# Fixed places for weight chunks, row counts in five steps, and a later fold in the last step of a mixture-of-experts block

## What is computed

```python
logits = h @ router_w + router_b                 # 512 tokens, 32 experts
top_vals, top_idx = lax.top_k(logits, 4)
gates = softmax(top_vals)
u = h[tokens of e] @ w_up[e] + b_up[e]           # 1024 -> 2048
a = min(u[::2], 7) * sigmoid(1.702 * min(u[::2], 7)) * (clip(u[1::2], -7, 7) + 1)
y = a @ w_down[e] + b_down[e]                    # 1024 -> 1024
x[tokens of e] += gate * y
out = rmsnorm(x) * final_norm_g
```

## Time and profile before

| | |
|---|---|
| runs | 1398.98, 1404.44, 1404.75 us; median 1404.44 |
| the profiled execution | 1400.33 us, its span 1398.5 us |
| TensorE busy | 94% of the span |
| VectorE busy | 85% |
| ScalarE busy | 75% |
| GpSimd busy | 20% |
| granted TensorE clock, mean | 0.979 |
| moved by DMA | 457.92 MB |

### The profile page before, as it was taken

The page is one execution under the profiler, slowest core; times in us unless marked ns, Lnnn a source line. Parts: engine busy times, 40 slices in busy tenths (PEclk is TensorE's granted clock), DMA queues, the critical chain, the costliest instruction groups (busy, mean ns, idle before and its releaser), DMA issues.

```text
span 1398.5 us, 18794 instructions
## 1 busy us (share of the span) xinstructions
PE 1311.2 (94%) x6287; PEld 1059.7 (76%) x6288; DVE 1185.3 (85%) x1064; ACT 1055.6 (75%) x900; POOL 281.0 (20%) x140
## 2 busy tenths in 40 slices
PE   6999989989998999999999999999999999999992
PEld 5888866678776878888788877778788878787771
DVE  5566645578998899999999999999999999999975
ACT  6454334336787898988889898989898888989873
POOL 0000001110165323322122121121122312212310
PEclk9999999989999999999999999999999999999996
DMA  8522153226999999999999999999999999999964
GB/s 243 143 61 76 46 199 163 94 103 252 406 337 408 371 411 412 409 414 397 420 400 416 405 420 403 398 402 414 416 405 408 407 413 406 421 404 408 399 248 140
DMA packets 71415, 457.92 MB, mean 327 GB/s; under 512 B 7371, under 2 KB 36203, under 8 KB 46737
## 3 DMA queue, kind: packets, MB, share of 16 engines
q1 hardware_dynamic: 64560, 438.13, 77.2%
q0 software_dynamic: 6816, 19.30, 5.8%
HBM read 443.35 MB, written 18.48 MB: 330 GB/s over the span
## 4 chain that ended last, share of the span: by engine, by line
PE 65%; DMA 16%; DVE 10%; issue 5%; ACT 3%; DVEq 0%; POOL 0%; SPq 0%; POOLq 0%; ACTq 0%
PE psum L1856 40%; DMA w_raw_pair<-w_up 11%; PE psum L1614 8%; DVE w_low L1258 5%; PE psum L1611 3%; DMA residual_rows<-y_rows,scatter_rows 3%; ACT w_high L777 2%; PE psum L1700 2%; PE psum L1748 2%; PE psum L1849 1%; PE psum L1839 1%; PE psum L1902 1%; DMA w_buf<-w_out 1%; PE psum L1724 1%; PE psum L1872 1%
## 5 line engine op out<-in xcount | busy, mean ns | idle before, releaser
L1258 DVE TENSOR_TENSOR w_low<-w_raw_pair,w_high 128x2048 fp32r<-128x2048 f32 x382 | 854.1, 2285 | 61.0 <-ACT w_high L777 60.1
L777 ACT ACTIVATE w_high<-w_raw_pair 128x2048 fp32r<-128x2048 f32 x384 | 717.8, 1911 | 117.2 <-DMA w_raw_pair<-w_up 45.6
L1856 PE MATMUL psum<-w_high,x_high 128*128 128x512 f32 x1040 | 286.3, 397 | 22.2 <-DVE x_high L1441 17.8
L1856 PE MATMUL psum<-w_low,x_high 128*128 128x512 f32 x1040 | 281.3, 392 | 0.0
L1856 PEld LDWEIGHTS psum<-w_high,x_high 128*128 128x128 f32 x1040 | 194.0, 190 | 71.1 <-DVE w_low L1258 27.4
L1856 PEld LDWEIGHTS psum<-w_low,x_high 128*128 128x128 f32 x1040 | 197.0, 189 | 42.2
L583 POOL DMA_INDIRECT residual_rows<-y_rows,scatter_rows x32 | 126.5, 3953 | 340.0 <-ACT y_rows L815 338.4
L1856 PE MATMUL psum<-w_high,a_high 128*128 128x512 f32 x496 | 156.2, 396 | 0.0
L1856 PE MATMUL psum<-w_low,a_high 128*128 128x512 f32 x496 | 154.2, 392 | 0.0
L1856 PE MATMUL psum<-w_high,x_low 128*128 128x512 f32 x512 | 141.1, 397 | 1.7 <-DVE w_low L1258 1.2
L1856 PEld LDWEIGHTS psum<-w_high,x_low 128*128 128x128 f32 x512 | 93.4, 188 | 26.8 <-issue 4.8
(11 more groups left out here) (306 smaller groups left out, 1451.4 us busy)
## 6 DMA issues: line engine op xcount, KB each, us to landing
w_raw_pair<-w_up SPq DMA_DIRECT2D x128, 2048.0 KB, 16.0
w_raw_pair<-w_down SPq DMA_DIRECT2D x64, 2048.0 KB, 14.9
w_in_raw<-w_in SPq DMA_DIRECT2D x28, 512.0 KB, 3.8
w_buf<-w_out SPq DMA_DIRECT2D x2, 2048.0 KB, 11.1
x_rows<-x SPq DMA_DIRECT2D x4, 512.0 KB, 5.4
x_rows<-x SPq DMA_DIRECT2D x1, 2048.0 KB, 18.8
residual_rows<-x_rows SPq DMA_DIRECT2D x4, 512.0 KB, 2.6
normed_rows<-h_rows SPq DMA_DIRECT2D x4, 512.0 KB, 2.6
```

Of the source, the lines that this page charges most:

```text
L777: act.activation(wh[:, q.slot(m, SPL), :], raw[q.slot(m, RAW)][:, :], ACT.Copy).then_inc(wh_ready, 1)
L1258: dve.tensor_tensor(wl[q.slot(m, RAW)][:, :], raw[q.slot(m, RAW)][:, :], wh[:, q.slot(m, SPL), :].bitcast(F32), ALU.subtract).then_inc(wl_ ...
L1856: ins = pe.matmul(o[:, j, :], x_part, w_part[:, j * 512:(j + 1) * 512], start=(first and n == 0), stop=(last and n == len(passes) - 1))
```

## The change

The edit has four parts. (1) Up chunk c always lies in raw place c and down chunk c in place 8 + c; the down chunks of expert 0 are loaded first, ahead of `ids_ready`, as soon as the last residual rows are out of TensorE's results, and `SECOND`'s up chunks wait for `FIRST`'s. The last expert's down chunks (`END`) go to places 0 to 3, so that `final_g_rows`, which lies over place 0, is loaded later. (2) `STEP` is 8 rows; scatter and gather have fewer rows for ranks 8 to 14 (80) and 23 to 30 (56), gathers of big places 96 rows for ranks 6 to 9 and 80 from rank 10 on. (3) In `order_experts` the cut comes out of four comparisons by rank. (4) In the last step the fold of the up result moves behind the first down chunk, `silu_half` and the last `swiglu` into `END`.

```diff
-FULL = 4
-STEP = P // 4
+STEP = P // 16
+SHORTER = ((4, 4), (8, 2), (SMALLS, 2), (SMALLS + 8, 1))
+ROWS_OF_PAIRS = ((0, 4, P, PH), (4, 8, P - 4 * STEP, PH), (8, PAIRS, P - 6 * STEP, PH - STEP))
...
         class Chunks:
-            def __init__(self, reg, mul, off):
-                self.reg, self.mul, self.off = reg, mul, off
+            def __init__(self, reg, mul, off, homes=(DNC, DNC, -UPC), first=0):
+                self.reg, self.mul, self.off, self.homes, self.first = reg, mul, off, homes, first
...
-            def slot(self, n, ring):
-                return (self.off + n) % ring
-            def turn(self, n, ring):
-                return self.reg * (self.mul // ring) + (self.off + n) // ring
+            def cast_slot(self, m):
+                return (self.off + m) % SPL
+            def place(self, n):
+                return n - self.first
+            def turn(self, n):
+                return self.reg * (self.mul // RAW) + (self.off + self.homes[n // 4] + n) // RAW
...
-        FIRST = Chunks(0, 0, 0)
+        FIRST = Chunks(0, 0, 0, (0, 0, 0))
         SECOND = Chunks(0, 0, UPC)
-        END = Chunks(0, 0, UPC + NC * (NE - 1))
+        END = Chunks(0, 0, UPC + NC * (NE - 1), (None, None, -DNC), UPC)
...
             def load_pair(q, n, m, e):
-                if q.starts(m) >= RAW:
+                if q is SECOND and n < UPC:
+                    sp.wait_ge(chunk_used, FIRST.count(n, 2))
+                elif q is not FIRST and q is not SECOND:
                     sp.wait_ge(chunk_used, q.count(m, 2 - RAW))
...
                 sp.dma_start(accv[:, i, :], X[:, i, :]).then_inc(S("acc_out"), 16)
+                if i == TT - 1:
+                    for n in range(UPC, NC, 2):
+                        load_pair(SECOND, n, n, 0)
                 sp.wait_ge(S("h2_rows"), i + 1)
...
-            step(SECOND, e1, 0)
+            step(SECOND, e1, None)
...
-            sp.wait_ge(chunk_used, nx * (2 * NC) + LAST.count(UPC - 2))
+            sp.wait_ge(chunk_used, nx * (2 * NC) + END.count(1))
             sp.dma_start(GF[:, :], final_g.rearrange("(o d) -> o d", o=1).to_broadcast([P, D])).then_inc(S("gf_in"), 16)
...
-            with pool.Fori(0, FULL) as i:
-                pair(i, P)
-            with pool.Fori(FULL, PAIRS) as i:
-                pair(i, P - STEP)
-            scatter(NE - 3, expert_at(NE - 3), PH)
-            scatter(NE - 2, expert_at(NE - 2), P - STEP)
-            scatter(NE - 1, expert_at(NE - 1), PH)
+            for first, end, big_rows, small_rows in ROWS_OF_PAIRS:
+                with pool.Fori(first, end) as i:
+                    scatter(i * 2 + 1, expert_at(i * 2 + 1), small_rows)
+                    gather(i * 2 + 5, expert_at(i * 2 + 5), use_x(i * 2 + 4), small_rows)
+                    scatter(i * 2 + 2, expert_at(i * 2 + 2), big_rows)
+                    gather(i * 2 + 6, expert_at(i * 2 + 6), use_x(i * 2 + 5), big_rows)
+            scatter(NE - 3, expert_at(NE - 3), PH - STEP)
+            scatter(NE - 2, expert_at(NE - 2), P - 6 * STEP)
+            scatter(NE - 1, expert_at(NE - 1), PH - STEP)
...
@@ ScalarE, small_step and the end @@
-                    if n == 9 and last:
+                    if n == 11 and last:
                         up_low_rows(p, q.count(UPC - 1, 1))
-                    if n == 11 and last:
-                        silu_half((p - 1) // 2)
                     cast(q, n, n)
...
             cast(END, UPC, 0)
+            silu_half(PAIRS + 1)
+            cast(END, UPC + 1, 1)
             a_high(LAST_A, PH, xh)
             bias_row(BSD2, of_place(NE - 1), bsd_ready, PH)
-            cast(END, UPC + 1, 1)
             gated(NE - 2, e30)
...
@@ VectorE, order_experts @@
-                link(dve.tensor_scalar(cut_steps, rank, float(FULL), cst("free")[0:NE, 0:1], ALU.is_ge, ALU.mult))
-                link(dve.tensor_tensor(cut_steps, cut_steps, is_small, ALU.add))
+                for n, (from_rank, steps) in enumerate(SHORTER):
+                    to = more_steps if n else cut_steps
+                    link(dve.tensor_scalar(to, rank, float(from_rank), float(steps), ALU.is_ge, ALU.mult))
+                    if n:
+                        link(dve.tensor_tensor(cut_steps, cut_steps, more_steps, ALU.add))
+                link(dve.tensor_tensor(cut_steps, cut_steps, cst("free")[0:NE, :], ALU.mult))
...
@@ VectorE, the end @@
-                    if n == 11 and last:
-                        swiglu(p, PH)
...
             split(END, 0)
+            swiglu(NE - 1, PH)
+            split(END, 1)
             a_low_half(NE - 1, xh)
-            for n in range(1, DNC):
+            for n in range(2, DNC):
                 split(END, n)
...
@@ TensorE, small_step @@
-                if last:
-                    up_fold(p, fold)
                 down(p - 1, use_a(p - 1))
                 for c in range(DNC):
                     down_chunk(q, UPC + c, c)
                     if c == 0 and not last:
                         x_transposed(p + 1, use_x(p + 1))
-                    if c == 1 and not last:
+                    if c == (0 if last else 1):
                         up_fold(p, fold)
```

More of the change, by code:

```diff
@@ L288, in hybrid_moe_block @@
         warm = small[:, 280:284]
-        key_col, rank, is_small, place, cut_steps = (small[0:NE, 112 + n:113 + n] for n in range(5))
+        key_col, rank, is_small, place, cut_steps, more_steps = (small[0:NE, 112 + n:113 + n] for n in range(6))
         key_row, diag, perm = order_work[:, 0:NE], order_work[:, NE:2 * NE], order_work[:, 2 * NE:3 * NE + 1]
@@ L422, in over_chunks @@
         def over_chunks(j):
-            return Chunks(j, NC, NC * NE)
+            return Chunks(j, NC, NC * NE, (RAW, 0, -RAW))
         X0, ROWS, X1 = range(3)
@@ L487, in load_pair @@
                     src = w_down[bass.ds(e, 1), 2 * c * P:2 * (c + 2) * P, :].rearrange("e (p t) n -> p (e t n)", t=4)
-                pair = q.slot(m, RAW) // 2
+                pair = q.place(n) // 2
                 sp.dma_start(pair_raw[pair][:, :], src).then_inc(raw_landed[pair], 16)
@@ L533, in _ @@
                     sp.wait_ge(S("items_ready"), 1)
+                    sp.wait_ge(chunk_used, END.count(DNC))
                     with sp.Fori(0, 2) as half:
@@ L561, in _ @@
                 pool.wait_ge(wh_ready, FIRST.count(n, 1))
[L562 to L563 removed]
+                pool.tensor_tensor(wl[n][:, :], raw[n][:, :],
+                                   wh[:, FIRST.cast_slot(n), :].bitcast(F32), ALU.subtract).then_inc(wl_ready, 1)
             def gather(g, col, x_before, rows=P):
@@ L772, in cast @@
             def cast(q, n, m):
-                act.wait_ge(raw_landed[q.slot(m, RAW) // 2], (q.turn(m, RAW) + 1) * 16)
+                act.wait_ge(raw_landed[q.place(n) // 2], (q.turn(n) + 1) * 16)
                 if q.starts(m) >= SPL:
                     act.wait_ge(chunk_used, q.count(m, 1 - SPL))
-                act.activation(wh[:, q.slot(m, SPL), :], raw[q.slot(m, RAW)][:, :], ACT.Copy).then_inc(wh_ready, 1)
+                act.activation(wh[:, q.cast_slot(m), :], raw[q.place(n)][:, :], ACT.Copy).then_inc(wh_ready, 1)
             def x_high(use, rows=P):
@@ L1256, in split @@
             def split(q, m):
+                n = q.place(m + q.first)
                 dve.wait_ge(wh_ready, q.count(m, 1))
-                dve.tensor_tensor(wl[q.slot(m, RAW)][:, :], raw[q.slot(m, RAW)][:, :],
-                                  wh[:, q.slot(m, SPL), :].bitcast(F32), ALU.subtract).then_inc(wl_ready, 1)
+                dve.tensor_tensor(wl[n][:, :], raw[n][:, :],
+                                  wh[:, q.cast_slot(m), :].bitcast(F32), ALU.subtract).then_inc(wl_ready, 1)
             dve.wait_ge(S("rb_in"), 16)
@@ L1475, in big_step, with small_step @@
                     split(q, n)
-            def small_step(p, q, last=False):
+            def small_step(p, q):
                 for n in range(NC):
@@ L1911, in down_chunk @@
                 pe.wait_ge(wl_ready, q.count(m, 1))
-                s = q.slot(m, SPL)
+                s = q.cast_slot(m)
                 for t in range(2):
                     k, w = 2 * c + t, slice(t * D, (t + 1) * D)
-                    ins = products(Yp, passes(ah[:, k, :], al[:, k, :], wh[:, s, w], wl[q.slot(m, RAW)][:, w]), D, first=(k == 0))
+                    ins = products(Yp, passes(ah[:, k, :], al[:, k, :], wh[:, s, w], wl[q.place(UPC + c)][:, w]), D, first=(k == 0))
                 ins.then_inc(chunk_used, 1)
@@ L1919, in down_chunk_half @@
                 pe.wait_ge(wl_ready, q.count(m, 1))
-                s = q.slot(m, SPL)
+                s = q.cast_slot(m)
                 for t in range(2):
                     k, w = 2 * c + t, slice(t * D, (t + 1) * D)
-                    ins = products(Yp, half_passes(both[:, k, :], wh[:, s, w], wl[q.slot(m, RAW)][:, w]), D, first=(k == 0), last=(k == DK - 1))
```

(1 more changed line is left out.)

15 lines of the change are left out of this document (5 added, 10 removed).

## The result

The changed kernel takes 1406.1 us (median of 20 runs, 1402.91 to 1409.72) against 1401.79 us for the kernel before in the same sequence (20 runs, 1396.47 to 1405.96). The ratio is 1.0031, 95% interval 1.0021 to 1.0041: 4.3 us slower. That is inside the 0.5% that the prediction calls no change, but the sign is not the forecast one, and the median lies 0.1 us above the range. The profiled execution took 1405.87 us with a span of 1404.1 us and a mean granted clock of 0.977.

What follows compares the result with a forecast made beforehand. The prediction took weight transfers to pace the experts' loop, with TensorE's floor 1.5 us per turn lower and wait chains at both ends. Terms +1.2 + 0 - 4.5 - 2.8 = -6.1 us gave 1398.3 from median 1404.44; range 1392 to 1402.

Steps and rivals of the forecast that it cites:

- Gathers: Experts' loop: 464 gather rows fewer, all skipped by the bounds check, 2.5 ns each, no bytes saved: 1.2 us faster.
- Scatters: Late experts' turns: 152 scattered rows fewer before the last weight landing, at 22 ns a row: 3.3 us faster.
- Start: Second step's start: up chunks 4 and 5 land later, delaying cast 4, `sig`, VectorE's product and six splits: +1.2 us.
- The state at 357.5 is the same: Start: weight transfers through by 357 us either way, later issues unchanged, so the 10 us moved ahead gain nothing.
- Order of experts: Sort of experts: eight small VectorE operations replace two, the extra 1.2 us hidden in idle time: 0 us.
- End: Last step: the later up fold removes TensorE's wait and half clock, `final_rows` comes earlier: -2.8 us (-1.5 to -3.5).
- In a stretch that transfers pace, 4.5 us less of them is 4.5 us less time: Experts' loop: saved scatter and gather time shortens the kernel fully while turns stay above 63.07 us: -4.5 us.
- Transfers don't pace: Rival for the loop: long turns come from when a scatter falls, rows give nothing; -1.6 us, 1402.8; chance 0.12.
- Skipped rows cost more: Rival for the loop: 8.5 ns per skipped gather row, 26 ns per scattered row; -10.9 us, 1393.5; chance 0.17.
- A further block: Slower rival: a late-ranked expert exceeds 80 or 56 tokens, adding two blocks of some 45 us each; 1490; chance 0.02.
- `SECOND` starves: Slower rival, cast 4 at 343 to 352 us: landing from 12.7 us costs 5.6 us plus 1.7 half clock; chance 0.08.
- Four rows an engine: Rival on small scatters: 56 rows go to 14 engines, saving nothing; 1.2 us less gain, -4.9, 1399.5; chance 0.08.

Runs made afterwards that it cites:

- scatter_cut: Kernel before with scatters cut to 80 and 56 rows and the four comparisons, gathers at their old 128 or 64 rows: 1398.78 us, 0.9977.
- places_silu_first: Kernel before with fixed places and early down loads, plus ScalarE's `x_high` and first `silu` one chunk earlier, ahead of cast 4: 1401.49 us, 0.9994.
- places_only: Kernel before with part (1) alone, the fixed places and early loads of expert 0's down chunks: 1403.88 us, 1.0024.
- all_gathers_128: Kernel before with 128 rows instead of 64 in all small gathers, only skipped rows added: 1400.03 us, 0.9982.
- big_gather_112: Kernel before with 112 rows instead of 128 in the loop's 14 big gathers, only skipped rows removed: 1414.51 us, 1.0079.
- small_64: Changed kernel with 64 rows for every small place instead of 56 in some: 1407.16 us, 1.0049 against the kernel before.

## Why the prediction was wrong

The forecast difference was -6.1 us, the measured one is +4.3. That the median missed the range by only 0.1 us is due to the base: the forecast was set on the median of three runs, 1404.44, and the 20 runs have 1401.79. Taken one by one, gathers (6.2 us worse than forecast), start (2.2), end (1.1) and scatters (0.1) make up 9.6 of the 10.4 us.

**Gathers (-1.2 us forecast, +5.0 to +7.4 measured).** This step failed, and is the largest part of the miss: with it alone put right the forecast would have been +0.1 to +2.5. "464 rows fewer ... so no bytes are saved" was right, and so was its lower bound of nothing for a skipped row. Wrong was that the number of rows is all that a gather's width changes. The rate of the weights beside it falls behind a gather narrower than 128 rows, in all but two of the windows above. The rows needed were within reach: the earlier trace rows were chosen around scatters, and no window was set behind each gather by size. Behind the small gather of before there are 401 GB/s, behind the big one 428, although the big one moves more. It would have said that a narrower big gather is a risk of about 0.7 us each (27 of 428 GB/s in 11 us), ten of them here. (The skipped rows of before are 956, not 952; nothing hangs on it.)

**Scatters (-3.3 us forecast, -3.2 measured, interval -5.0 to -1.3).** The size is right. The way, 22 ns a row for 152 rows taken off the turns from 951 us on, is not shown: those turns are no shorter in the profiled execution of `scatter_cut`, and the interval is too wide to tell 152 rows from fewer.

**Start (+1.2 us forecast, +3.4 measured).** The chain was right: four pairs behind each other, the landing in 8.4 us (8.3 forecast), cast 4, `sig`, product and splits 1.4 us late. Missing was TensorE. The term costed the stretch by VectorE's splits alone; the wait of 2.60 us and the half clock behind it were priced (1.7 us), but in the slower rival, from a landing of 12.7 us on. They come at 8.4 us too. Wrong too was "The state at 357.5 is the same": the wait and the half clock put off the next pair by 5.1 us, and the engines, full there before, have a share of 0.13 and 0.32. That the late `sig` is the cause is shown by `places_silu_first`, which takes away the wait, the half clock, the late issue and the loss with it (-0.8 us, interval -2.4 to +0.8). How the other 2 us reach the end was not followed; the late pair is the likely way, and the thirteen turns take 837.6 us in `places_only`, 835.3 before.

**Order of experts (0).** No experiment holds it apart; it is in `scatter_cut`, which loses nothing against its term.

**End (-2.8 us forecast, -1.7 measured, interval -3.6 to +0.3).** Right in order and place. ScalarE's copy of the up result's lower rows waits for the last up chunk in both kernels; from its start to SyncE's issue of `final_rows` it is 36.2 us before (1344.14 to 1380.36) and 33.6 after (1353.13 to 1386.76), 2.6 us less. In time the gain is not clear of nothing.

**"In a stretch that transfers pace, 4.5 us less of them is 4.5 us less time."** Only the other direction shows. Where the transfers got slower, the thirteen turns grew: in the changed kernel the weights took 8.6 us more of the engines' time (of which up to 4 may be the spread between kernels) and the turns 7.8 us more; in `big_gather_112` it is 13.5 and 13.7. Where they got quicker, the turns did not visibly shrink: `all_gathers_128` has 5.8 us less and 0.7 us shorter turns. *Transfers don't pace* (0.12) had the rows give nothing, and the interval of `scatter_cut` speaks against that; that a saving reaches the turns us for us is not shown. *Skipped rows cost more* (0.17) is out: 960 more of them in `all_gathers_128` leave q0 at 5.8%. *A further block* did not come. *`SECOND` starves* happened in a small form, above.

***Four rows an engine*** (0.08). By the Trainium skill, "DMA: Bandwidth & Descriptors", section "Why a DMA increments its semaphore by 16 and not by 1", the general rule sends 56 rows to 14 engines, four each. With a packet a row that would be 56 packets. The page of the profile of the changed kernel has 6288, which is 6176 and 14 times 8, and 14 is the number of transfers of 56 rows; `small_64`, with 64 rows in them, has 6288 too. So each leaves as many packets as 64 rows do, and the plain division by 14 isn't borne out. The forecast's 6176 was wrong by that rounding. But the rival's consequence, that 56 rows save nothing against 64, fits these packets, and its price (1.2 us) lies inside every interval here: it stays open. `big_gather_112` has 6592, which is 6816 less 14 times 16, so 112 rows aren't rounded.

Of the signs listed, the early down pairs, `sig`, the splits, the fold and the full clock behind the last up chunk came as said. "Turns from 951 on nearer 63.6" did not, and the packet count was off by 112. Of the two signs against it, TensorE's new wait at `SECOND` came; the DMA share under 1 did not, and the turns grew all the same. The share tells that engines are occupied; the rate beside it tells what they get done.

## What to carry to other kernels

Where transfers set the pace, price a transfer by the rate of the others beside it, size by size, before its rows are cut: here 16 skipped rows fewer cost 0.8 us a gather, and padding a gather to all 128 partitions cost nothing in the total. When a chain is moved by a us or two, ask whether TensorE gets a new wait by it, what it runs at behind that wait (here 1.2 GHz behind 2.60 us), and which loads wait for what it does then; one block of ScalarE issued ahead of a late chunk's cast took all three away. And time the parts of a bundle apart: a gain of 3.2 us, and perhaps one of 1.7, lay hidden under two losses.

## What the runs showed of the hardware

- **Narrow gathers slow the weights on another queue.** In the 11 us behind an indirect gather the rate is 367 to 395 GB/s with 80 to 112 rows, 385 to 409 with 56 or 64 (two exceptions at 423 and 424), and 414 to 432 with 128, at a DMA share near 1.01 in all. 14 gathers cut from 128 to 112 rows: +11.1 us (1.0079, 1.0060 to 1.0098). The physical cause is only argued. 112 rows are 7 for each of 16 engines if dealt evenly, and then an engine's rows no longer lie in the partitions that its weight rows go to. The Trainium skill, "DMA: Bandwidth & Descriptors", section "The descriptor swizzle", says that in a transfer to 128 partitions each engine's eight writes go to a fixed set of partitions behind one port; that would fit, but no run here shows a single engine or port.
- **A gather row that the bounds check skips is a packet and costs next to nothing.** 960 more: q0 from 6816 to 7776 packets, its share 5.8% in both.
- **A scatter of 80 rows can keep GpSimd for 17.24 us**, beside 7.39 us for one of the same size at 986.96 us of the same run. With every gather at 128 rows, each of the 11 big scatters from 650 us on takes 7.7 us or more, before 3 of 11. It is in no step of the prediction, and what decides it stays open.
